# The first norm of a two-block model, taken with the features on partitions: sums of squares by products with ones, inverse norms spread from a diagonal

## The reference

```python
def rmsnorm(x, g):
    xf = x.astype(jnp.float32)
    y = xf * lax.rsqrt(jnp.mean(xf * xf, axis=-1, keepdims=True) + RMS_EPS)
    return (y * g.astype(jnp.float32)).astype(x.dtype)
...
    for layer in range(DEPTH):
        h = rmsnorm(x, mix_pre_g[layer])
        if layer % 2 == 0:
            m = even_mixer(h, ...)          # proj = h @ w_in: f_logit, q, k, v, u
        ...
        x = x + rmsnorm(m, mix_post_g[layer])
```

## Time and profile before

| what | value |
|---|---|
| median of 3 runs | 3601.39 us (3601.29 to 3603.22) |
| the profiled execution's own time | 3603.33 us |
| its span in the profile | 3601.6 us |
| PE busy | 3401.8 us, 94% of the span |
| DVE, ACT, POOL busy | 48%, 21%, 41% |
| granted TensorE clock, mean | 0.979 of full |

### The profile page before, as it was taken

How to read it: one execution, slowest core, us unless ns; L and a number is a source line. 1 busy time by engine, 2 the same in 40 slices (tenths; PEclk the granted TensorE clock), 3 DMA queues, 4 the chain that set the end, 5 groups by cost and what they waited for, 6 DMA issues and landing times.

```text
span 3601.6 us, 39516 instructions
## 1 busy us (share of the span) xinstructions
PE 3401.8 (94%) x15717; PEld 2777.2 (77%) x15717; DVE 1732.8 (48%) x1806; ACT 767.0 (21%) x1122; POOL 1481.7 (41%) x723
## 2 busy tenths in 40 slices
PE   8999889999999999998999999999896999999997
PEld 7777678788888887777888888887775777767786
DVE  3444324433233258776423333258665566565542
ACT  4333322000000043344100000031121223222111
POOL 2211665334334455455443343355743222413264
PEclk9999899999999999999999999999998999999999
DMA  4110032111111131113111111133214110201133
GB/s 149 47 30 27 18 117 88 47 47 47 50 49 47 52 129 41 41 59 129 47 47 52 47 47 47 52 129 88 71 59 125 43 44 23 60 24 50 35 123 105
DMA packets 244366, 227.94 MB, mean 63 GB/s; under 512 B 8940, under 2 KB 206228, under 8 KB 244264
## 3 DMA queue, kind: packets, MB, share of 16 engines
q1 hardware_dynamic: 224480, 180.32, 16.6%
q10 hardware_dynamic: 19784, 46.22, 3.8%
HBM read 188.65 MB, written 33.64 MB: 62 GB/s over the span
## 4 chain that ended last, share of the span: by engine, by line
PE 73%; DVE 12%; issue 5%; POOL 4%; ACT 4%; ACTq 1%; DMA 1%; DVEq 0%; SPq 0%; POOLq 0%
PE ps L357 23%; PE ps L358 22%; PE ps L359 22%; PE ps L587 1%; DVE lru_xc L1599 1%; POOL w_hi L345 1%; POOL Y L666 1%; POOL w_lo L347 1%; PE ps L2406 1%; PE ps L1032 1%; DVE Y L712 1%; ACT b_junk L470 1%; ACTq L2041 1%; DVE ml_st_lo L2634 0%; PE ps L1912 0%
## 5 line engine op out<-in xcount | busy, mean ns | idle before, releaser
L345 POOL TENSOR_TENSOR w_hi<-raw,one_col 128x1024 fp32r<-128x1024 f32 x275 | 544.9, 1981 | 1830.6 <-PE ps L359 1806.7
L357 PE MATMUL ps<-H_hi,w_hi 128*128 128x512 f32 x2720 | 1085.3, 399 | 42.6 <-POOL w_lo L347 7.0
L359 PE MATMUL ps<-H_hi,w_lo 128*128 128x512 f32 x2720 | 1064.5, 391 | 0.0
L358 PE MATMUL ps<-H_lo,w_hi 128*128 128x512 f32 x2720 | 1063.9, 391 | 0.0
L347 POOL TENSOR_TENSOR w_lo<-raw,w_hi 128x1024 fp32r<-128x1024 f32 x275 | 697.5, 2536 | 21.6
L357 PEld LDWEIGHTS ps<-H_hi,w_hi 128*128 128x128 f32 x2720 | 514.0, 189 | 154.1 <-issue 21.7
L359 PEld LDWEIGHTS ps<-H_hi,w_lo 128*128 128x128 f32 x2720 | 513.5, 189 | 108.9
L358 PEld LDWEIGHTS ps<-H_lo,w_hi 128*128 128x128 f32 x2720 | 514.2, 189 | 101.6 <-issue 1.9
L359 PE MATMUL ps<-w_hi,ffn_f_lo 128*128 128x512 f32 x704 | 273.9, 389 | 0.0
L357 PE MATMUL ps<-w_hi,ffn_f_hi 128*128 128x512 f32 x704 | 273.9, 389 | 0.0
L358 PE MATMUL ps<-w_lo,ffn_f_hi 128*128 128x512 f32 x704 | 273.9, 389 | 0.0
(11 more groups left out here) (475 smaller groups left out, 4725.9 us busy)
## 6 DMA issues: line engine op xcount, KB each, us to landing
raw<-in_w_in SPq DMA_DIRECT2D x49, 512.0 KB
raw<-in_ffn_w_gate SPq DMA_DIRECT2D x44, 512.0 KB
raw<-in_ffn_w_up SPq DMA_DIRECT2D x44, 512.0 KB
raw<-in_ffn_w_down SPq DMA_DIRECT2D x44, 512.0 KB
b_X<-x_dram SPq DMA_DIRECT2D x24, 512.0 KB, 5.4
x_dram<-Y SPq DMA_DIRECT2D x24, 512.0 KB, 5.1
raw<-in_ev_w_in SPq DMA_DIRECT2D x17, 512.0 KB
x_dram<-Y ACTq DMA_DIRECT2D x16, 512.0 KB, 3.6
```

The costliest lines, as they stand in the source:

```text
L345: pool.tensor_tensor(w_hi[s][:, :n], raw[s][:, :n], one_col[:, :].broadcast_to([P, n]), ALU.mult).then_inc(split_hi, 1)
L357: pe.matmul(o, l_hi, r_hi, start=first, stop=False)
L358: pe.matmul(o, l_hi, r_lo, start=False, stop=False)
L359: return pe.matmul(o, l_lo, r_hi, start=False, stop=last)
```

## The change

The squares' sums no longer come from turned tiles. In the changed kernel ACT squares `XT` as it stands (`x_sq`, in three pieces of 3, 3 and 2 feature tiles, as they are loaded), and PE sums over the partitions by 32 products of a 128x128 piece of `x_sq` as the weights with a single column of ones (event `sums`). ACT takes four roots at once, DVE inverts and builds the four diagonals, and PE multiplies a 128x128 matrix of ones by each diagonal (`spread`), which puts the inverse norm of every token on all partitions of one PSUM bank. DVE multiplies `XT` by that bank (`scaled`, which writes PSUM), and `high` and `low` follow as before. For the second half the sums still come from turned tiles (ACT, `tile_square`), but all four are made before its `spread`.

The turned tiles are now needed for the residual only. Tiles 0 and 1 are turned around the first `spread`, tiles 4 to 7 between the products of the first half, tiles 2 and 3 behind the first and the second chunk of the second half. ACT copies tiles 0, 1, 4 and 6, DVE 5, 7, 2 and 3. The stores go to SP's queue in the order 0, 1, 4, 5, 6, 7, 2, 3. SP loads the first weight chunk ahead of x, and chunks k0 and v0 ahead of the stores. The first table load of ACT moves ahead of the gain rows, and POOL's split of v0 moves from `fox` into the boundary.

```diff
+            x_sq = nc.alloc_sbuf_tensor_at(f"{tag}_x_sq", [P, KT, HALF], F32, offset=tmp_at + 53248)
+            pieces = (slice(0, 3), slice(3, 6), slice(6, 8))
+            pe_order = ("sums", 0, "spread0", 1, 4, 5, 6, 7, "spread1", 2, 3)
+            act_copies, dve_copies = (0, 1, 4, 6), (5, 7, 2, 3)
...
+        def tile_copied(e, i):
+            if i in act_copies:
+                wait(e, "x_made", act_copies.index(i) + 1)
+            else:
+                wait(e, "x_made_dve", dve_copies.index(i) + 1)
+
+        def pe_done(e, event):
+            wait(e, "tile_done", pe_order.index(event) + 1)
...
-            return (2, 0, 1)[i] if i < 3 else 2
+            return {1: 1, 2: 3, 3: 3}.get(i, 2)
...
-                for h in range(2):
-                    e.dma_start(XT[:, :, halves[h]], A["x_t"][:, :, halves[h]].rearrange("k p n -> p k n")).then_inc(q[f"x{h}"], 16)
-                    if h == 0:
-                        load_chunks(e, seam[0], seam[1], seam[1] + 2)
+                load_chunks(e, seam[0], seam[1], seam[1] + 1)
+                for j, ks in enumerate(pieces):
+                    e.dma_start(XT[:, ks, halves[0]], A["x_t"][ks, :, halves[0]].rearrange("k p n -> p k n")).then_inc(q[f"x{j}"], 16)
+                load_chunks(e, seam[0], seam[1] + 1, seam[1] + 2)
+                wait(e, "x0", 16)
+                e.dma_start(XT[:, :, halves[1]], A["x_t"][:, :, halves[1]].rearrange("k p n -> p k n")).then_inc(q["x0"], 16)
+                load_chunks(e, seam[0], seam[1] + 2, seam[1] + 4)
+                for i in (0, 1, 4, 5, 6, 7, 2, 3):
+                    tile_copied(e, i)
+                    e.dma_start(x_dram[i, :, :], Y[:, i, :]).then_inc(q["x_stored"], 16)
...
-                for i in range(4):
-                    x_root(i)
-                    if i:
-                        diagonal(i - 1)
-                diagonal(3)
-                for k in range(5):
-                    high(0, k)
-                for i in range(4):
-                    store(i)
-                for i in range(4, KT):
-                    x_root(i)
-                    if i + 1 < KT:
-                        high(0, i + 1)
-                    if i > 4:
-                        diagonal(i - 1)
-                diagonal(KT - 1)
+                def copy(i):
+                    pe_done(e, i)
+                    e.activation(Y[:, i, :], pair(entry_pair(i)), ACT.Copy).then_inc(q["x_made"], 1)
+
+                def tile_square(i):
+                    tile_copied(e, i)
+                    wait(e, "squared", i - 1)
+                    e.activation(junk[:, :], Y[:, i, :], ACT.Square, accum_out=entry(3, i)).then_inc(q["squared"], 1)
+
+                def roots(h, sums):
+                    e.activation(stat[:, 4 * KT + 4 * h:4 * KT + 4 * h + 4], sums, ACT.Sqrt, scale=1.0 / D, bias=eps_col[:, :]).then_inc(q["x_root"], 1)
+
+                for j, ks in enumerate(pieces):
+                    wait(e, f"x{j}", 16)
+                    e.activation(x_sq[:, ks, :], XT[:, ks, halves[0]], ACT.Square).then_inc(q["squared"], 1)
+                pe_done(e, "sums")
+                roots(0, ps[:, 0:4, 0])
+                copy(0)
+                high(0, 0)
+                copy(1)
+                high(0, 1)
+                high(0, 2)
+                high(0, 3)
+                copy(4)
+                high(0, 4)
+                tile_square(4)
+                high(0, 5)
+                tile_square(5)
+                high(0, 6)
+                high(0, 7)
+                copy(6)
+                tile_square(6)
+                tile_square(7)
+                wait(e, "squared", 7)
+                roots(1, stat[:, 3 * KT + 4:4 * KT])
                 for k in range(KT):
                     high(1, k)
-                    if k < 4:
-                        store(k + 4)
...
-            def token_tile(i):
-                wait(e, f"x{i // 4}", 16)
-                if i >= 3:
-                    wait(e, "x_made", 1 if i == 3 else i)
+            if not post:
+                def token_tile(i):
+                    for k in range(KT):
+                        ins = e.transpose(pair(entry_pair(i))[:, k * P:(k + 1) * P], XT[:, k, i * P:(i + 1) * P], ident[:, :])
+                    ins.then_inc(q["tile_done"], 1)
+
+                def spread(h):
+                    wait(e, "turn_ready", 4 * h + 4)
+                    for i in range(4):
+                        ins = e.matmul(ps[:, 1 + 2 * h, i * P:(i + 1) * P], ones[:, :], diag[:, 4 * h + i, :], start=True, stop=True)
+                    ins.then_inc(q["tile_done"], 1)
+
+                for j, ks in enumerate(pieces):
+                    wait(e, "squared", j + 1)
+                    for k in range(ks.start, ks.stop):
+                        for i in range(4):
+                            ins = e.matmul(ps[:, i, 0:1], x_sq[:, k, i * P:(i + 1) * P], ones[:, 0:1], start=k == 0, stop=k == KT - 1)
+                ins.then_inc(q["tile_done"], 1)
+                token_tile(0)
+                spread(0)
+                token_tile(1)
                 for k in range(KT):
-                    ins = e.transpose(pair(entry_pair(i))[:, k * P:(k + 1) * P], XT[:, k, i * P:(i + 1) * P], ident[:, :])
-                ins.then_inc(q["tile_done"], 1)
-
-            if not post:
-                for i in range(4):
-                    token_tile(i)
+                    wait(e, "h_low", k + 1)
+                    for c in range(2):
+                        if k == 0:
+                            ready(c)
+                            if c == 1:
+                                wait(e, "x_made", 2)
+                        step(0, c, k)
+                    if k == 1:
+                        wait(e, "x0", 32)
+                        wait(e, "x_made", 1)
+                        token_tile(4)
+                    elif k == 3:
+                        wait(e, "x_made", 3)
+                        token_tile(5)
+                    elif k == 5:
+                        wait(e, "x_made_dve", 1)
+                        token_tile(6)
+                    elif k == 6:
+                        wait(e, "x_made", 4)
+                        token_tile(7)
+                wait(e, "x_made_dve", 2)
+                ready(2)
+                for k in range(KT):
+                    step(0, 2, k)
+                    if k == 2:
+                        spread(1)
+                for c in range(3):
+                    for k in range(KT):
+                        wait(e, "h_low", KT + k + 1)
+                        ins = step(1, c, k)
+                    ins.then_inc(multiplied, 1)
+                    if c == 0:
+                        token_tile(2)
+                    elif c == 1:
+                        wait(e, "x_made_dve", 3)
+                        token_tile(3)
+                wait(e, "x_made_dve", 4)
+                return
...
-                splits(0, 3)
+                splits(0, 4)
...
+                    e.tensor_copy(Y[:, i, :], pair(entry_pair(i))).then_inc(q["x_made_dve"], 1)
+
+                def diagonals(h):
+                    wait(e, "x_root", h + 1)
+                    o(e.reciprocal(stat[:, 5 * KT + 4 * h:5 * KT + 4 * h + 4], stat[:, 4 * KT + 4 * h:4 * KT + 4 * h + 4]))
+                    for i in range(4 * h, 4 * h + 4):
+                        e.tensor_scalar(diag[:, i, :], ident[:, :], entry(5, i), None, ALU.mult).then_inc(q["turn_ready"], 1)
+
+                def scaled(h, k):
+                    if k == 0:
+                        pe_done(e, f"spread{h}")
+                    if KT * h + k >= 2:
+                        wait(e, "h_low", KT * h + k - 1)
+                    e.tensor_tensor(ps[:, 6 + k % 2, :], XT[:, k, halves[h]], ps[:, 1 + 2 * h, :], ALU.mult).then_inc(q["turned"], 1)
+
+                diagonals(0)
+                scaled(0, 0)
+                for k in range(KT):
+                    if k + 1 < KT:
+                        scaled(0, k + 1)
                     low(0, k)
-                for i in range(4, KT):
-                    copy(i)
-                    low(0, i)
-                    if i > 4:
-                        turning(i - 1)
-                turning(KT - 1)
+                    if k == 5:
+                        copy(5)
+                copy(7)
+                diagonals(1)
+                scaled(1, 0)
                 for k in range(KT):
+                    if k + 1 < KT:
+                        scaled(1, k + 1)
                     low(1, k)
+                copy(2)
+                copy(3)
...
+            e.activation(warm[:, :], eps_col[:, :], ACT.Sqrt)
...
-            load_chunks(e, N, 2, 4)
...
-            split_chunks(e, N, SLOTS, chunk["u2"] + 1)
+            split_chunks(e, N, SLOTS + 1, chunk["u2"] + 1)
```

20 lines of the change are left out of this document (5 added, 15 removed).

## The result

The changed kernel takes 3614.66 us (median of 7 runs, 3612.04 to 3617.46), the one before 3601.29 (7 runs beside them, 3600.78 to 3603.22): a ratio of 1.0034, 95% interval 1.0024 to 1.0043. It is slower by 13.4 us, 6.5 more than the 6.8 of the forecast, and 3614.66 lies outside the range. Measured twice more, the same kernel gave 3614.3 and 3616.25, beside 3601.74 and 3602.6 for the one before. The profiled execution of the changed kernel is the fastest of its seven (3612.04, span 3610.2), so against the profile before it shows 8.6 us.

The account below looks back on a forecast made before the run. PE, busy 94% of the span, was taken as the bound. The start's terms put the filler at 97.4: 97.4 − 91.5 + 0.9 = +6.8 us, on 3601.4 giving 3608.2, range 3600.5 to 3611.

Parts of the forecast that it names:

- Loads and squares: Start of the kernel: first piece of x lands at about 8.2 us instead of 10.2, PE may begin sums at 9.85.
- Sums: PE's sums over the partitions at the start: 64 weight loads at 0.21 us each, 13.5 us, ending at 23.4.
- To the first product: From the sums through root, diagonals, `spread`, `scaled`, `high`, `low`: 5.9 us, first product at 29.3 against 26.5.
- First half, second half: Boundary products: first half 16.2 us with 1.4 waiting on tile 5; second at DVE's pace, chunk f done at 62.7.
- The seam: Boundary to attention: `f_abs` waits for tile 3's store until 74.1, 8.8 later than before; filler starts at 97.4.
- Clock at the filler: Start of the filler: lower clock level lasts 0 to 1.0 us more after the longer idle, taken as 0.9.
- Rivals 2, 3 and 5: Clock rises during sums, 3603.3 (chance 0.20); load costs 0.11 to 0.12, 3602.0 (0.12); store's wait not holding `f_abs`, 3600.7 (0.06).
- Rival 4: First products after the sums: clock still low, 0.43 a matmul instead of 0.23, +1.8 us, 3610.0; chance 0.14.
- all behind it is unchanged and should shift with it: Everything behind the filler's start, which is 91.50 before the change, was taken to move only with that start.

Follow-up runs that it names:

- s3: The changed kernel with the squares and the column of ones of the sums in bf16, 32 weight loads in place of 64: 3603.92 us, ratio 1.0007.
- g1: The changed kernel with `f_abs` free of the last two stores and DVE adding the eight squared tiles before PE sums: 3604.82 us, ratio 1.0009.
- a3: The changed kernel with 103 idle PE instructions, 44 ahead of the sums and 59 before the filler, restoring the code's earlier place: 3609.07 us, ratio 1.002.

## Why the prediction was wrong, and where it was right

The mechanism at the start and at the seam was right, step by step:

- *Loads and squares*: the first piece at 8.8 (forecast 8.2), the sums from 10.34 (9.85).
- *Sums*: 13.8 us (13.5). The forecast's 0.21 a record was right (0.216), 0.11 wrong. What doubles it is PE's pace at the start: the eight weight loads of `spread` took 1.78 us at 26.3 and 0.97 at 49.0 in the same trace, though the clock column shows 1.00 in both places. The moving side does not, since one and two columns cost the same. The Trainium skill, "TensorE: Matmul & The Clock Gate", section "LDWEIGHTS (loading the stationary operand)", gives columns / 1.2 ns, 107 ns for 128 columns; the trace agrees at 49 us (0.12) and has twice that at the start. A stream of such sums at the fast pace is in no run.
- *To the first product*: 6.5 us after the sums (5.9); 30.67 (29.3).
- *First half, second half*: tile 5's copy cost PE 0.5 instead of 1.4, and the second half came at DVE's pace of 1.39 (1.45): chunk f done at 62.5 (62.7).
- *The seam*: `f_abs` at 73.7 (74.1), filler at 97.0 (97.4), 5.5 us late (5.9), held by `w_lo`.
- *Clock at the filler*, 0.9: up to 529 us the offset stays 5.3, so this term was nought in the first profile. In the two later ones of the changed kernel the products at 500 us are 7.7 and 7.5 late, 1.8 and 1.4 more than the filler was: the bounds of 0 to 1.0 were too narrow.
- A slip without weight: the terms of the first half, 10.9, 3.6 and 1.4, make 15.9, not 16.2.
- Rivals 2, 3 and 5 are out. Rival 4 is out for this kernel (the first product is 0.50 long), and came true in s3 and g1, whose sums give PE less to do before the first product.

The step that failed is the sentence "all behind it is unchanged and should shift with it". The work behind the filler is unchanged; its instructions stand elsewhere in PE's code. PE ran 32291 instructions instead of 32394, the pieces of its code were fetched at other moments, and seven of them fell on a DMA issue of ACT's. Each such issue is 0.5 to 0.9 us longer in the first profile; PE waits for the data or the buffer behind it, and a longer wait can lengthen a stretch at the lower clock, as at 530 us (0.85 became 2.1). The forecast of +6.8 had nothing for this; the seam came out as forecast, 5.5 instead of 5.9, and behind the filler stand 7.9 us where it had 0.9. Of the 7.0 us between its profile and a3's, 3.1 arise from 530 to 647 us and 3.6 in s5.

Shown is that the code's place alone brings this and takes it away: the reverse run puts 8.3 us into the kernel before, 103 idle instructions take 7.2 out of the changed one, a whole piece of 256 doesn't. The two traces side by side show that nearly all of it arises behind slow issues and the low clock that follows them. Not shown is why ACT's issue waits while PE's code is fetched, and how the 3.6 us in s5 divide between the late issues and the clock. The 0 to 3 us behind the filler in kernels without a slow issue are of the size by which executions of one program differ with their clock; they were not taken apart further.

The Trainium skill, "Runtime: NRT & Kernel Launch", section "Instruction fetch mechanics", says that code is refilled in blocks of 16 KiB, 256 instructions, and that crossing a boundary is mostly hidden. The pieces agree with the trace (packets of 0.02 MB, and the run with 256 instructions more). "Hidden" holds for PE as far as the traces tell: a3 and the changed kernel fetch their pieces at different instructions and from 647 to 2550 us, over more than twenty packets, the distance between them ends up only 0.4 larger. It does not hold for ACT.

## What to carry to other kernels

When a change alters how many instructions an engine runs, every later piece of its code is fetched at another moment, and some microseconds can come or go in stages that nobody touched; so compare the time up to a marker behind the changed stage apart from the time behind it, and if the latter moved, look at the longest issue among equal ones before giving it to the clock. Ask of each buffer's or store's semaphore what is queued behind the engine that waits for it: here one late store held `f_abs` for 11 us and the filler for 6.3, and two semaphores in place of one gave them back. Before giving DVE work "because it is idle", see whether POOL is busy at that time.
